# A second projection: unit loads ahead of the bias stores, token tiles' steps in another order

## The chip, the cores and the metric

One core of a Trainium2 chip runs the whole program. The metric is the device time of one execution in microseconds. The engines are TensorE (PE; PEld is its weight load), VectorE (DVE), ScalarE (ACT), GpSimd (POOL) and SyncE (SP), which here issues nearly all transfers from one queue, in program order.

## What is computed

Two transformer blocks on 512 tokens of width 1024, in fp32. The first block is a projection, stick-breaking attention and a recurrent scan, and a mixture of 32 experts; the second takes its normed output, projects it to queries, keys, values and gates, and does windowed attention. What matters here lies between the two:

```python
h = h + y.reshape(B, S, D)              # experts' rows are added
x = rmsnorm(h, final_norm_g)            # end of the first block
h = rms_norm(x, norm_gain[layer])       # start of the second
proj = h @ w_in[layer]                  # 1024 x 8448
qa, ka, va, qb, kb, vb, ga, gb, mg = jnp.split(proj, split_idx, axis=-1)
bias = bias_table[t5_bucket(rel * stride)]    # relative position bias of the attention
```

## The kernel before

The stage at issue is the class `SecondProjection`. Its weights come in 21 units of 256 columns and 1 MB each. Each is loaded raw by SyncE, then split into a high part (ScalarE, L653) and a low part (VectorE, L661), and TensorE multiplies three products of the parts (high by high, high by low, low by high). Unit 0 has a raw room of its own; the others alternate between two rooms, so that the load of unit n waits until the low part of unit n - 2 is made. The parts alternate between two rooms also, but unit 2 has a third one.

Ahead of that the tokens are prepared in four tiles of 128. For each tile c the rows of the two chosen experts are loaded into `yg` (1 MB, L2222), added to `h` in two additions (`add(c, 0)`, `add(c, 1)`, L2390, VectorE), squared and summed (`square(c)`, L2324, ScalarE), weighed with the squared gains (`weigh(c)`, L2395, VectorE), and turned into a diagonal of scales (`scale(c)`, to L2408, VectorE, with two roots on ScalarE). TensorE then turns the tile with it (`turn(c)`, L2245, 16 matmuls), ScalarE makes eight high parts (`highs(c)`, L2338) and VectorE eight low parts (`low(c)`, L2413). TensorE multiplies tile by tile with units 0 and 1 (24 matmuls of 256 columns each, L2274); within unit 1, behind 18 of its 24 matmuls, stands the turning of the next tile. Then come units 2 to 20 one by one for all 512 tokens: two jobs of 24 x 2 or 24 matmuls each (L603), and after a job with a head norm two matmuls of head sums.

The bias rows (`BiasRows`) are made beside this: SyncE loads tables, TensorE picks rows of them (L2096), VectorE adds the windows (`add_windows`, L2105), SyncE stores them in four copies of 256 KB (`store`, L2112), from where attention reads them later. They lie in `qk_a`, the room of the first normed queries, so that VectorE waits for their landing before it writes there.

The order on every engine is that of the code: each engine's method issues its instructions one after the other, and a waiting instruction holds all behind it. On SyncE the method `sync` issues the units' loads, the row loads, the stores of the bias rows and four stores of values (L2233) in one line. On ScalarE and VectorE the splits of a unit stand at chosen places between the tiles' steps.

Of the kernel before, what the change touches and what calls it, by code (L numbers as in the profile page):

```python
# [17 lines left out]
TT = S // P  # L18
# [2129 lines left out]
class SecondProjection:  # L2148
# [65 lines left out]
    def sync(self, sp, rows_written):  # L2214
        T, wts, const = self.T, self.wts, self.const
        w, cols = second_columns(self.A)
        sp.dma_start(wts.slot(0), w[:, :, cols[0]:cols[0] + UNIT]).then_inc(const["second_w_in"], 16)
        sp.dma_start(self.fin_g[:, :], self.A["final_norm_g"].rearrange("(a d) -> a d", a=1).broadcast_to([P, D])).then_inc(self.gain_in, 16)
        wts.load(sp, 1)
        sp.wait_ge(*rows_written)  # L2220
        for c in range(TT):
            sp.dma_start(self.yg[c], self.rows[c]).then_inc(self.got[c], 16)  # L2222
        self.bias.load(sp)
        v_rows = T["v_dram"].rearrange("(c p) w -> p c w", p=P)
        early = 2 * HW // UNIT
        for u in range(2, len(wts.cols)):
            wts.load(sp, u)
            if u == 2:
                self.bias.store(sp)
            if 3 <= u < early + 3:  # L2230
                at = slice((u - 3) * UNIT, (u - 2) * UNIT)
                sp.wait_ge(self.v_st, self.plain.index(self.last_job[u - 3]) + 1)
                sp.dma_start(v_rows[:, :, at], T["v12"][:, :, at]).then_inc(T["v12_written"], 16)  # L2233
            if u == early + 4:
                sp.wait_ge(T["v12_written"], 16 * early)
                sp.wait_ge(self.bias.stored, 64)
                load_bias(sp, const, T["band0"], 0, 0, 3 * P, T["band0_in"])
# [76 lines left out]
    def scalar(self, act):  # L2314
        jobs, normed, bank, wts, const, sq, rs = self.jobs, self.normed, self.bank, self.wts, self.const, self.sq, self.rs
        act.preload_act_table(ACT.Sqrt)
        for u in range(self.EARLY):
            wts.split_high(act, u)

        def square(c):  # L2320
            act.wait_ge(self.added, 2 * c + 2)
            if c >= 2:
                act.wait_ge(self.weighed, c - 1)
            act.activation(self.h_sq[c % 2], self.h[:, c, :], ACT.Square, accum_out=self.ss[:, c:c + 1]).then_inc(self.squared, 1)  # L2324

        def highs(c):
            act.wait_ge(self.fin, 3 * c + 2)
            act.activation(self.ws[:, c:c + 1], self.ws[:, c:c + 1], ACT.Sqrt).then_inc(self.root, 1)
            act.wait_ge(self.fin, 3 * c + 3)
            act.activation(const["fin_rstd"][:, c:c + 1], self.inv[:, c:c + 1], ACT.Sqrt).then_inc(self.root, 1)  # L2330
            if c == 0:
                act.wait_ge(self.gains_made, 1)
            for k in range(KC):
                if k < self.NTURN:
                    act.wait_ge(self.turned, self.NTURN * c + k + 1)
                else:
                    act.wait_ge(self.low_st, KC * c + k - self.NTURN + 1)
                act.activation(self.hT[0][:, k, c * P:(c + 1) * P], self.turn_at(k), ACT.Copy, scale=self.fin_cols[:, k:k + 1]).then_inc(self.high_st, 1)  # L2338

        square(0)  # L2340
        for c in range(TT):
            if c + 1 < TT:
                square(c + 1)
            highs(c)
        act.preload_act_table_set("natural_log_exp_and_others")
        wts.split_high(act, self.EARLY)

        def factors(i):

            act.wait_ge(self.summed, i + 1)  # L2350
            if i >= 2:
                act.wait_ge(self.qk_st, i - 1)
            act.activation(rs[:, i % 2, :], self.sums[i % 2][:, :], ACT.Ln, scale=1.0 / HD, bias=const["eps"][:, :]).then_inc(self.logged, 1)
            act.wait_ge(self.logged, i + 1)
            act.activation(rs[:, i % 2, :], rs[:, i % 2, :], ACT.Exp, scale=-0.5).then_inc(self.rstd, 1)

        for n, (u, kind, x, dst, gain, perm) in enumerate(jobs):
            act.wait_ge(self.ready, n + 1)
            if n in normed:
                i = normed.index(n)  # L2360
                if i >= 2:
                    act.wait_ge(self.summed, i - 1)
                act.activation(sq[:, i % 2, :], bank[n % self.NBANK][:, :], ACT.Square).then_inc(self.hn_squared, 1)
                act.wait_ge(self.hn_squared, i + 1)
                act.activation(self.sq_part[0][:, i % 2, :], sq[:, i % 2, :], ACT.Copy).then_inc(self.sq_high, 1)  # L2365
            else:
                width = P if kind == "va" else UNIT
                act.activation(dst, bank[n % self.NBANK][:, :].rearrange("p (c w) -> p c w", w=width), ACT.Copy).then_inc(self.v_st, 1)
            if u >= self.EARLY and self.last_job.get(u - 1) == n - 1:
                wts.split_high(act, u + 1)  # L2370
            if n - 1 in normed:
                factors(normed.index(n - 1))
# [8 lines left out]
    def vector(self, dve):  # L2381
# [3 lines left out]
        def add(c, j):  # L2385
            if j == 0:
                dve.wait_ge(self.got[c], 16)
            else:
                dve.wait_ge(self.added, 2 * c + 1)
            dve.scalar_tensor_tensor(out=self.h[:, c, :], in0=self.yg[c][:, j, :], scalar=self.weights[:, j, c:c + 1], in1=self.h[:, c, :],  # L2390
                                     op0=ALU.mult, op1=ALU.add).then_inc(self.added, 1)
# [27 lines left out]
        wts.split_low(dve, 0)  # L2419
        dve.wait_ge(self.gain_in, 16)  # L2420
        dve.tensor_tensor(self.gain_sq, self.fin_g[:, :], self.fin_g[:, :], ALU.mult).then_inc(self.gained, 1)
        wts.split_low(dve, 1)
        dve.wait_ge(self.gained, 1)

        for c in range(2):
            for j in range(2):
                add(c, j)
        weigh(0)
        for c in range(TT):
            scale(c)  # L2430
            if c + 2 < TT:
                add(c + 2, 0)
            elif c + 1 < TT:
                weigh(c + 1)
            low(c)
            if c + 2 < TT:
                add(c + 2, 1)
                weigh(c + 1)
        wts.split_low(dve, self.EARLY)
        for c in range(TT):  # L2440
            dve.tensor_tensor(self.h[:, c, :], self.h[:, c, :], self.fin_g[:, :], ALU.mult).then_inc(self.gained, 1)
        self.bias.add_windows(dve)
        dve.wait_ge(self.bias.stored, 64)
        for m, (u, *_) in enumerate(jobs):
            if u >= self.EARLY and self.last_job.get(u - 1) == m - 1:
                wts.split_low(dve, u + 1)
# [2 lines left out]
                continue  # L2449
            u, kind, x, dst, gain, perm = jobs[n]  # L2450
            i = normed.index(n)
            dve.wait_ge(self.rstd, i + 1)
            r = rs[:, i % 2, :]
            dve.tensor_scalar(r, r, gains[:, gain:gain + 1], None, ALU.mult).then_inc(self.hn_gained, 1)
# [797 lines left out]
```

## Time and profile before

| | |
|---|---|
| median of 3 timed runs | 1354.25 us (1352.88 to 1354.81) |
| the profiled execution | 1351.7 us |
| its span, first to last instruction | 1350.0 us |
| TensorE busy | 1230.9 us, 91% of the span |
| TensorE weight loads busy | 967.8 us, 72% |
| VectorE busy | 559.8 us, 41% |
| ScalarE busy | 492.2 us, 36% |
| GpSimd busy | 153.8 us, 11% |

TensorE is the busy engine; a time gained or lost is one in which it stands still or runs at the lower clock. Busy shares are means over stages with different limits, so the stage at issue, from about 710 to 830 us, has to be read on its own: what TensorE waited for in it, and what that waited for.

### The profile page before, as it was taken

Reading aid. Unit: us, or ns where it says so; the run is one execution under the profiler, and the core shown is the slowest. Engines: PE = TensorE matmul, PEld = TensorE weight load, DVE = VectorE, ACT = ScalarE, POOL = GpSimd, SP = SyncE. Lnnn points to the kernel's source line nnn. Section 1 sums busy time; section 2 is a strip of 40 time slices with the busy share of each in tenths; the row PEclk is TensorE's granted clock in tenths of the full one; section 3 lists DMA queues with packets and bytes.
Section 4 is the critical chain, followed back from the end, with each engine's and each line's share of the span. In section 5 each row is a group of like instructions: output and inputs, shape, how many; then the busy total and the mean of one; then the engine's idle time right before and its main releaser. Section 6 shows DMA issues by size and latency. Waiting matters only on the chain. (4 is left out here: it accounts for less than half of the span.)

```text
span 1350.0 us, 24557 instructions
## 1 busy us (share of the span) xinstructions
PE 1230.9 (91%) x10443; PEld 967.8 (72%) x10443; DVE 559.8 (41%) x1018; ACT 492.2 (36%) x881; POOL 153.8 (11%) x210
## 2 busy tenths in 40 slices
PE   5999999999979779999782939999999999999988
PEld 5787765699858546565442938888896678888888
DVE  3433563345373323333226602344446773553242
ACT  4324537602243311111113414455546663332230
POOL 4000013200000011111100001122210015300000
PEclk9999999999999979999996969999999999999999
DMA  4431000000029699999987064422216118222031
GB/s 157 122 104 63 32 1 0 9 5 4 15 72 408 235 368 417 418 418 418 418 368 247 6 167 126 96 90 94 94 32 95 64 34 281 63 63 94 0 109 48
DMA packets 92679, 197.63 MB, mean 146 GB/s; under 512 B 9694, under 2 KB 73276, under 8 KB 79644
## 3 DMA queue, kind: packets, MB, share of 16 engines
q1 hardware_dynamic: 87244, 185.58, 39.2%
q0 software_dynamic: 4752, 8.40, 1.6%
q10 hardware_dynamic: 576, 2.10, 0.4%
q8 instruction: 83, 1.36, 0.4%
q14 instruction: 24, 0.20, 0.0%
HBM read 186.06 MB, written 17.86 MB: 151 GB/s over the span
## 5 line engine op out<-in xcount | busy, mean ns | idle before, releaser
L661 DVE TENSOR_TENSOR w_in_low<-w_in_raw,w_in_high 128x2048 fp32r<-128x2048 f32 x19 | 43.6, 2293 | 122.1 <-ACT w_in_high L653 122.1
L1945 PE MATMUL hidden_ps<-w_gate,gathered_t 128*64 128x256 f32 x384 | 90.4, 389 | 0.3 <-DVE gathered_t L2022 0.3
L1945 PE MATMUL hidden_ps<-w_up,gathered_t 128*64 128x256 f32 x384 | 90.3, 389 | 0.0
L1487 PE MATMUL wo_ps<-w_out_high,wo_x_high 128*128 128x256 f32 x256 | 74.2, 290 | 3.5 <-DVE w_out_low L672 3.5
L2862 PE MATMUL gate_ps<-block_in_high,gate_w_high 128*128 128x512 f32 x192 | 75.9, 395 | 1.0 <-PEq L2531 1.0
L2862 PE MATMUL gate_ps<-block_in_high,gate_w_low 128*128 128x512 f32 x192 | 74.9, 390 | 0.0
L2862 PE MATMUL gate_ps<-block_in_low,gate_w_high 128*128 128x512 f32 x192 | 74.8, 390 | 0.0
L1487 PE MATMUL wo_ps<-w_out_high,wo_x_low 128*128 128x256 f32 x256 | 73.1, 285 | 0.0
L1487 PE MATMUL wo_ps<-w_out_low,wo_x_high 128*128 128x256 f32 x256 | 73.0, 285 | 0.0
L1945 PEld LDWEIGHTS hidden_ps<-w_gate,gathered_t 128*64 128x64 f32 x384 | 51.6, 139 | 27.6 <-issue 2.1
L2379 POOL TENSOR_TENSOR qk_sq_low<-y_a_b,qk_sq_high 128x512 fp32r<-128x512 f32 x29 | 37.5, 1294 | 247.2 <-ACT qk_sq_high L2365 247.2
L603 PE MATMUL u_ps<-mixer_in_high,w_in_high 128*128 128x512 f32 x160 | 63.7, 398 | 1.7 <-DVE w_in_low L661 1.7
L603 PE MATMUL u_ps<-mixer_in_low,w_in_high 128*128 128x512 f32 x160 | 62.3, 390 | 0.0
L603 PE MATMUL u_ps<-mixer_in_high,w_in_low 128*128 128x512 f32 x160 | 62.3, 389 | 0.0
L2002 ACT ACTIVATE silu<-hidden_ps 64x256 f32<-64x256 f32 x32 | 12.0, 375 | 137.6 <-PE hidden_ps L1945 137.6
L1967 PE MATMUL expert_ps<-w_down,hidden 128*64 128x512 f32 x216 | 51.3, 595 | 8.9 <-issue 6.5
L2048 DVE TENSOR_TENSOR hidden_t<-hidden_ps,silu 64x256 f32<-64x256 f32 x32 | 13.7, 427 | 108.5 <-ACT silu L2002 108.5
L1487 PEld LDWEIGHTS wo_ps<-w_out_high,wo_x_high 128*128 128x128 f32 x256 | 49.5, 194 | 8.9 <-issue 5.0
L1945 PEld LDWEIGHTS hidden_ps<-w_up,gathered_t 128*64 128x64 f32 x384 | 51.6, 139 | 0.0
L1487 PEld LDWEIGHTS wo_ps<-w_out_high,wo_x_low 128*128 128x128 f32 x256 | 49.9, 195 | 0.0
L1487 PEld LDWEIGHTS wo_ps<-w_out_low,wo_x_high 128*128 128x128 f32 x256 | 49.5, 194 | 0.0
L653 ACT ACTIVATE w_in_high<-w_in_raw 128x2048 fp32r<-128x2048 f32 x19 | 36.2, 1903 | 24.4 <-DMA w_in_raw<-w_in_dram 24.4
(531 smaller groups left out, 3250.4 us busy)
## 6 DMA issues: line engine op xcount, KB each, us to landing
w_down<-exp_w_down_dram SPq DMA_DIRECT2D x27, 1024.0 KB, 28.0
w_gate<-exp_w_gate_dram SPq DMA_DIRECT2D x24, 1024.0 KB, 22.5
w_up<-exp_w_up_dram SPq DMA_DIRECT2D x24, 1024.0 KB, 25.1
w_in_raw<-w_in_dram SPq DMA_DIRECT2D x20, 1024.0 KB, 5.6
slot_scratch_and_keys<-w_in_dram SPq DMA_DIRECT2D x14, 1024.0 KB, 5.2
vb<-w_in_dram SPq DMA_DIRECT2D x6, 1024.0 KB, 5.7
gate_w_raw_odd<-w_in_dram SPq DMA_DIRECT2D x6, 1024.0 KB, 6.4
slot_scratch_and_keys<-exp_w_down_dram SPq DMA_DIRECT2D x5, 1024.0 KB, 30.6
```

The lines of the kernel that those rows point to most:

```text
L603: m = pe.matmul(out, a(k)[i], b(k)[j], start=(k == 0 and i + j == 0), stop=(k == n - 1 and i == 1))
L653: act.activation(self.part[0][self.at(n)], self.slot(n), ACT.Copy).then_inc(self.high, 1)
L661: dve.tensor_tensor(self.part[1][self.at(n)], self.slot(n), self.part[0][self.at(n)], ALU.subtract).then_inc(self.low, 1)
L1487: m = pe.matmul(banks[n % nb][:, 0:UNIT], x[a][k][:, c * P:(c + 1) * P], wts.parts(u, k, slice(0, UNIT))[b], start=(k == 0 and a + b == 0) ...
L1945: x = pe.matmul(g_bank[e % 2][a * CAP:(a + 1) * CAP, 0:DE], xT[e % 2][:, k, :], w[:, k, :], start=(k == 0), stop=(k == KC - 1))
L1967: x = pe.matmul(y_bank[e % 2][half * CAP:(half + 1) * CAP, :], hid[e % 2][:, f, :], wd[e % NBD][:, f, half * 512:(half + 1) * 512], start= ...
L2002: act.activation(act_g[e % 2][CAP:P, :], g_bank[e % 2][0:CAP, 0:DE], ACT.Silu).then_inc(silu, 1)
L2048: dve.tensor_tensor(hid_t[e % 2][CAP:P, :], g_bank[e % 2][CAP:P, 0:DE], act_g[e % 2][CAP:P, :], ALU.mult).then_inc(mul_r, 1)
L2379: pool.tensor_tensor(self.sq_part[1][:, 0, :], self.sq[:, i % 2, :], self.sq_part[0][:, i % 2, :], ALU.subtract).then_inc(self.sq_low, 1)
L2862: m = pe.matmul(bank[n % NBANK][:, :], wts.parts(unit, k, w)[a], hT[b][:, k, :], start=(k == 0 and a + b == 0), stop=(k == KC - 1 and a == 1))
```

## The change

It moves instructions and adds none. On SyncE the load of unit 1 goes behind the first row load, and the stores of the bias rows go from behind unit 2's load to behind unit 4's. On ScalarE the high part of unit 1 goes behind tile 0's high parts, and the square of tile c + 1 behind the high parts of tile c. On VectorE the second addition of tile c + 1 and its weighing go behind the low parts of tile c (for tile 1 the addition stays ahead of them), and unit 1's low part goes behind tile 0's. VectorE's wait for the bias rows' landing goes from behind the windows to ahead of the first head norm.

```diff
--- before.py
+++ after.py
@@ -2216,16 +2216,17 @@
         w, cols = second_columns(self.A)
         sp.dma_start(wts.slot(0), w[:, :, cols[0]:cols[0] + UNIT]).then_inc(const["second_w_in"], 16)
         sp.dma_start(self.fin_g[:, :], self.A["final_norm_g"].rearrange("(a d) -> a d", a=1).broadcast_to([P, D])).then_inc(self.gain_in, 16)
-        wts.load(sp, 1)
         sp.wait_ge(*rows_written)
         for c in range(TT):
             sp.dma_start(self.yg[c], self.rows[c]).then_inc(self.got[c], 16)
+            if c == 0:
+                wts.load(sp, 1)
         self.bias.load(sp)
         v_rows = T["v_dram"].rearrange("(c p) w -> p c w", p=P)
         early = 2 * HW // UNIT
         for u in range(2, len(wts.cols)):
             wts.load(sp, u)
-            if u == 2:
+            if u == self.EARLY + 2:
                 self.bias.store(sp)
             if 3 <= u < early + 3:
                 at = slice((u - 3) * UNIT, (u - 2) * UNIT)
@@ -2314,8 +2315,7 @@
     def scalar(self, act):
         jobs, normed, bank, wts, const, sq, rs = self.jobs, self.normed, self.bank, self.wts, self.const, self.sq, self.rs
         act.preload_act_table(ACT.Sqrt)
-        for u in range(self.EARLY):
-            wts.split_high(act, u)
+        wts.split_high(act, 0)
 
         def square(c):
             act.wait_ge(self.added, 2 * c + 2)
@@ -2339,9 +2339,11 @@
 
         square(0)
         for c in range(TT):
-            if c + 1 < TT:
-                square(c + 1)
+            if c:
+                square(c)
             highs(c)
+            if c == 0:
+                wts.split_high(act, 1)
         act.preload_act_table_set("natural_log_exp_and_others")
         wts.split_high(act, self.EARLY)
 
@@ -2419,28 +2421,28 @@
         wts.split_low(dve, 0)
         dve.wait_ge(self.gain_in, 16)
         dve.tensor_tensor(self.gain_sq, self.fin_g[:, :], self.fin_g[:, :], ALU.mult).then_inc(self.gained, 1)
+        dve.wait_ge(self.gained, 1)
+
+        add(0, 0)
+        add(0, 1)
+        add(1, 0)
+        weigh(0)
+        scale(0)
+        add(1, 1)
+        low(0)
         wts.split_low(dve, 1)
-        dve.wait_ge(self.gained, 1)
-
-        for c in range(2):
-            for j in range(2):
-                add(c, j)
-        weigh(0)
-        for c in range(TT):
+        for c in range(1, TT):
+            weigh(c)
             scale(c)
-            if c + 2 < TT:
-                add(c + 2, 0)
-            elif c + 1 < TT:
-                weigh(c + 1)
+            if c + 1 < TT:
+                add(c + 1, 0)
             low(c)
-            if c + 2 < TT:
-                add(c + 2, 1)
-                weigh(c + 1)
+            if c + 1 < TT:
+                add(c + 1, 1)
         wts.split_low(dve, self.EARLY)
         for c in range(TT):
             dve.tensor_tensor(self.h[:, c, :], self.h[:, c, :], self.fin_g[:, :], ALU.mult).then_inc(self.gained, 1)
         self.bias.add_windows(dve)
-        dve.wait_ge(self.bias.stored, 64)
         for m, (u, *_) in enumerate(jobs):
             if u >= self.EARLY and self.last_job.get(u - 1) == m - 1:
                 wts.split_low(dve, u + 1)
@@ -2449,6 +2451,8 @@
                 continue
             u, kind, x, dst, gain, perm = jobs[n]
             i = normed.index(n)
+            if i == 0:
+                dve.wait_ge(self.bias.stored, 64)
             dve.wait_ge(self.rstd, i + 1)
             r = rs[:, i % 2, :]
             dve.tensor_scalar(r, r, gains[:, gain:gain + 1], None, ALU.mult).then_inc(self.hn_gained, 1)
```

SyncE at the row loads: `slot_scratch_and_keys` holds raw unit 0, `w_in_raw` the later raw units, `qb` and `vb` the experts' rows (`yg`).

```order
 L2218 DMA final_gain<-final_norm_g_dram 128x1024
-L642 DMA w_in_raw<-w_in_dram 128x8x256
-L2220 REGISTER_ALU
-L2222 DMA qb<-expert_rows_dram 128x2048 x3
-L2222 DMA vb<-expert_rows_dram 128x2048
+L2219 REGISTER_ALU
+L2221 DMA qb<-expert_rows_dram 128x2048
+L642 DMA w_in_raw<-w_in_dram 128x8x256
+L2221 DMA qb<-expert_rows_dram 128x2048 x2
+L2221 DMA vb<-expert_rows_dram 128x2048
```

The load of unit 1 moved from ahead of the wait for the experts' rows to between the first and the second row load.

SyncE behind the bias tables' loads: `bias_rows_dram` are the bias rows' stores, `class_v_dram` the values' stores.

```order
 L2091 DMA sink<-sink_a_dram 128x8
+L642 DMA w_in_raw<-w_in_dram 128x8x256 x2
+L2234 DMA class_v_dram<-vb 128x4x256
 L642 DMA w_in_raw<-w_in_dram 128x8x256
 L2112 DMA bias_rows_dram<-qk_a 128x1x512 x4
```

Units 2, 3 and 4 and the first values' store now stand ahead of the bias rows' stores, where only unit 2 stood.

VectorE between the low parts of tile 0 and of tile 1: `block_in_low` are the tokens' low parts, `h<-` the additions, the ISA rows the weighing, `y_a_b<-ident` the diagonal for turning. Before:

```order
L2413 SCALAR_TENSOR_TENSOR block_in_low<-expert_ps,final_gain_columns,block_in_high 128x128 x2
L2390 SCALAR_TENSOR_TENSOR h<-qb,route_weights,h 128x1024
L2395 ISA vb,fin_weighted<-vb 128x1024
L2395 ISA fin_weighted 128x1
L2400 TENSOR_SCALAR fin_squares<-fin_squares 128x1
```

Of the change:

```order
L2415 SCALAR_TENSOR_TENSOR block_in_low<-expert_ps,final_gain_columns,block_in_high 128x128 x2
L661 TENSOR_TENSOR w_in_low<-w_in_raw,w_in_high 128x2048
L2397 ISA vb,fin_weighted<-vb 128x1024
L2397 ISA fin_weighted 128x1
L2402 TENSOR_SCALAR fin_squares<-fin_squares 128x1
```

Unit 1's low part, which stood ahead of the first addition, now stands behind tile 0's low parts and ahead of tile 1's weighing, and the addition of tile 2 there has gone behind the diagonal.

## Rows read from the trace of the kernel before

**Rows 1.** Waits of TensorE, whole run: instruction, what it waited for: us, times, longest.

```profile
PE hidden_ps L603 <- DVE w_in_low L661: 20.8, 1, 20.8
```

**Rows 2.** Timeline of SyncE: start, us, engine, line, operation, output<-input, count.

```profile
718.38 1.29 SPq L2222 DMA_DIRECT2D qb<-expert_rows_dram  x3
...
771.58 10.05 SPq L2112 DMA_DIRECT2D bias_rows_dram<-qk_a  x4
781.67 3.78 SPq L642 DMA_DIRECT2D w_in_raw<-w_in_dram  x1
```

**Rows 3.** Timeline of ScalarE, units 2 to 5; in brackets: idle before it, releaser.

```profile
772.57 0.60 ACT L2368 ACTIVATE vb<-expert_ps 128x512 f32<-128x512 f32 x1 [4.86 <-PE expert_ps L603]
794.37 1.91 ACT L653 ACTIVATE w_in_high<-w_in_raw 128x2048 fp32r<-128x2048 f32 x1 [21.20 <-DMA w_in_raw<-w_in_dram]
...
807.17 0.60 ACT L2368 ACTIVATE vb<-hidden_ps 128x512 f32<-128x512 f32 x1 [10.41 <-PE hidden_ps L603]
...
812.93 0.60 ACT L2368 ACTIVATE vb<-hidden_ps 128x512 f32<-128x512 f32 x1 [3.37 <-PE hidden_ps L603]
818.40 0.60 ACT L2363 ACTIVATE y_a_b<-hidden_turned_ps 128x512 f32<-128x512 f32 x1 [4.87 <-PE hidden_turned_ps L603]
...
819.56 1.90 ACT L653 ACTIVATE w_in_high<-w_in_raw 128x2048 fp32r<-128x2048 f32 x1
```

**Rows 4.** Timeline of VectorE, bias windows and unit 3.

```profile
770.29 1.27 DVE L2105 TENSOR_TENSOR qk_a<-gathered_ps,qk_a 16x512 f32<-16x512 f32 x2
796.40 2.29 DVE L661 TENSOR_TENSOR w_in_low<-w_in_raw,w_in_high 128x2048 fp32r<-128x2048 f32 x1 [24.85 <-ACT w_in_high L653]
```

**Rows 5.** Stretch of the stores: us, TensorE busy (matmuls), clock, DMA share, GB/s.

```profile
776.00:778.00 2.00, 1.97 (x18) 1.00 0.44 48
```

**Rows 6.** DMA issues near 781, 718.4 and 718.9 us: count, size, us to landing.

```profile
w_in_raw<-w_in_dram SPq DMA_DIRECT2D x1, 1024.0 KB, 12.6
...
qb<-expert_rows_dram SPq DMA_DIRECT2D x1, 1024.0 KB, 6.1
...
qb<-expert_rows_dram SPq DMA_DIRECT2D x1, 1024.0 KB, 8.2
```

**Rows 7.** Timeline of VectorE, tiles 0 and 1.

```profile
725.09 5.12 DVE L2390 SCALAR_TENSOR_TENSOR h<-qb,route_weights,h 128x1024 f32<-128x1024 f32 x4
730.12 1.22 DVE L2395 CUSTOM_DVE_ANT_0 vb<-vb 128x1024 f32<-128x1024 f32 x1
...
739.09 1.22 DVE L2395 CUSTOM_DVE_ANT_0 vb<-vb 128x1024 f32<-128x1024 f32 x1
...
744.74 0.60 DVE L2413 SCALAR_TENSOR_TENSOR block_in_low<-expert_ps,final_gain_columns,block_in_high 128x128 fp32r<-128x128 f32 x2
```

**Rows 8.** Timeline of TensorE: the first matmuls of the turns of tiles 0 to 2.

```profile
732.49 2.08 PE L2245 MATMUL gathered_ps<-y_a_b,h 128*128 128x128 f32 x8 [23.40 <-DVE y_a_b L2408]
...
741.46 1.16 PE L2245 MATMUL gathered_ps<-y_a_b,h 128*128 128x128 f32 x8 [0.24 <-DVE y_a_b L2408]
...
749.11 1.05 PE L2245 MATMUL gathered_ps<-y_a_b,h 128*128 128x128 f32 x8
```

**Rows 9.** Timeline of ScalarE, tile 0's last high parts, a later square.

```profile
736.96 0.64 ACT L2338 ACTIVATE block_in_high<-expert_ps,final_gain_columns 128x128 fp32r<-128x128 f32 x2
...
746.57 1.06 ACT L2324 ACTIVATE vb<-h 128x1024 f32<-128x1024 f32 x1 [1.61 <-DVE h L2390]
747.53 0.19 ACT L2324 ACTIVATION_READ_ACCUMULATOR vb<-h 128x1 f32 x1
```

**Rows 10.** TensorE behind two gaps (timeline), and the stretches there (columns of rows 5).

```profile
398.34 2.05 PE L593 MATMUL wo_ps<-heads 128*128 128x128 f32 x8 [3.01 <-PEq L102]
...
463.56 0.43 PE L1657 MATMUL router_in_ps<-ident,router_in_t 36*128 36x36 f32 x4 [2.56 <-DVE router_in_t L1680]
...
398.00:399.00 1.00, 0.66 (x3) 0.50 0.00 0
463.00:464.00 1.00, 0.43 (x4) 1.00 0.98 406
```

## The prediction

> **What bounds the kernel now.** I read first the table of waits of TensorE over the whole run. Its second-longest entry is 20.8 us, once, in the first matmul of a weight unit of the second projection: it waits for VectorE's low part [rows 1]. To see what that wait hangs on I followed it back through three timelines. VectorE makes the low part of unit 3 at 796.40 [rows 4], ScalarE its high part at 794.37, after idling 21.2 us for the transfer of the raw unit [rows 3]. SyncE issues that transfer at 781.67, directly behind the four stores of the bias rows, which occupied it from 771.58 for 10.05 us [rows 2]. They were last released by VectorE's addition of the windows (770.29, two of them, 1.27 us together [rows 4]). The room that unit 3 is loaded into was free since unit 1's low part, before 725.09 [rows 7]. So the order on one queue holds TensorE, and nothing else does: that is what the change can win.
>
> **Part 1, unit 3 (and 4) ahead of the stores.** The load of unit 3 waits for two low parts, now made before tile 1 is turned; the load of unit 4 waits for unit 2's low part, made before the windows are added. Both are then on their way before 771.6 in the old times. What is late next? ScalarE has the copy of unit 2's first result at 772.57 [rows 3]; behind it comes unit 3's high part, 1.91 us [rows 3], and VectorE's low part, 2.29 us [rows 4], no longer behind the wait for the stores' landing, which the change moves to the first head norm. 772.6 + 0.6 + 1.9 + 2.3 = 777.4. TensorE ended unit 2 about 798.75 - 20.8 = 777.95. The 20.8 us go whole, with 0.5 us to spare.
>
> With them goes a cold start: unit 3's first job ran from 798.75 to 807.17, 8.4 us, the second, alike, took 812.93 - 807.17 = 5.76 us [rows 3]; the difference, 2.6 us, is gone if TensorE does not stop. Part 1 gives **-23.4 us**.
>
> What it delays is unit 5, now the first load behind the stores. Its need in old times: unit 3 ends at 777.95 + 2 x 5.76 = 789.5; unit 4's first job takes 818.40 - 812.93 = 5.47 [rows 3] and ends at 795.0; the high part starts 819.56 - 818.40 = 1.2 us later [rows 3], and could start 0.8 us later still, since TensorE has two head sums between unit 4 and unit 5. So unit 5 must have landed by 796.2 to 797.0. Unit 3's load took 12.6 us from its issue right behind the stores [rows 6], landing at 794.3. Ahead of unit 5's load there is half a megabyte more, a store of values; a megabyte took about 2.5 us on a busy queue (landings of 6.1 and 8.2 us for two row loads issued about 0.4 us apart [rows 6]), so 1.3 us more: 795.6. I cost this at **zero**, with 3 us as the other bound, the cover being 0.6 to 1.4 us.
>
> Why that load is slow shows in the stores' stretch: the DMA engines' mean busy share was 0.44 at 48 GB/s [rows 5]. By a rule of the Trainium skill (DMA: Bandwidth & Descriptors, Rules for kernel authors) a copy whose outermost dimension is under 16, here 8 heads, is confined to at most that many of the engines. The trace agrees, with a share just under a half; a load behind the stores must then wait on those engines, which speaks against putting any load there, and the change still leaves unit 5's.
>
> **Part 2, row loads.** Unit 1's load goes from before the wait on the experts' rows to behind the first row load. Tile 0's chain starts when the rows land. Before, the first was issued at 718.38 [rows 2] and landed 6.1 us later, at 724.5, the second 8.2 us after its issue, at 727.0 [rows 6]; VectorE added four half-rows from 725.09 and weighed at 730.12 [rows 7]. Now only three additions stand ahead, but the third needs the second row load, and unit 1's megabyte is between the two. Set against the old order the same bytes have moved when it lands, and the DMA engines stand idle while SyncE waits for the rows, for an estimated 1 to 2 us. So it lands at 727.0 + 1.3 = 728.3, addition three ends at 729.6, weighing starts then instead of 730.12: **-0.5 us**. Bounds: -1.8 (no idle time, 727.0) and +2.5 (the first row load still takes 6.1 us, then two megabytes at 2.5 us: 729.5, and up to 731.3 if unit 1's smaller packets run slower, which gives weighing at 732.6).
>
> **Part 3, tiles.** Let T be TensorE's first turning matmul, 732.49 now [rows 8]. Unit 1's split is no longer made before T but after tile 0's high parts on ScalarE and low parts on VectorE. The last high parts start at 736.96 and two more take 0.64 [rows 9], so they end at T + 5.1. ScalarE then takes 1.91 for unit 1 (T + 7.0), VectorE 2.29 (T + 9.3). TensorE had its 24 matmuls of unit 0 done at about T + 6.2 and must stand 3.1 us, which it did not before. VectorE goes on with tile 1: its weighing (ScalarE's square is done by T + 8.0) starts at T + 9.2. From weighing to turning takes 741.46 - 739.09 = 2.37 us [rows 7, 8] and 732.49 - 730.12 says the same. So tile 1 is turned at T + 11.6; before it was 741.46 - 732.49 = 8.97. **+2.6 us.**
>
> For tiles 2 and 3 the order is now turn, low parts, second addition, square, weigh, turn, in a chain without overlap, because the sum of a tile is completed only after the previous tile's low parts. Turn to low parts' end: 744.74 + 0.60 - 741.46 = 3.9 [rows 7, 8]. From there to weighing: addition 1.25 (four took 5.12 [rows 7]), square from 746.57 to 747.53 + 0.19 [rows 9], in all 2.4. Then 2.37. Sum 8.65 from turn to turn. Before it was 749.11 - 741.46 = 7.65 [rows 8], with TensorE busy throughout. Two such steps, of 1.0 and (the old step to tile 3 was 0.1 shorter) 1.1: **+2.1 us**. Behind the last turn all goes as before, shifted. Part 3 is 4.7 us.
>
> **Part 4, the clock.** A gap of 3.01 us in this trace was followed by a stretch at a granted clock of 0.50, the 1.2 GHz level; one of 2.56 us was not (1.00, 2.4 GHz) [rows 10]. The new gap of 3.1 us is on the side of the first. I take it that the clock falls. The 18 matmuls of unit 1 before the turn need 18/64 of a 7.6 us step, 2.1 us, and twice that at the lower level; TensorE then reaches the turn at T + 13.5 instead of T + 11.6: **+2.0 us** (bounds 0, and 2.6, what the first job lost after 20.8 us of idling).
>
> The Trainium skill (TensorE: Matmul & The Clock Gate, Part 1: The HAM clock gate) says that the point of change varies from run to run, since the gate's phase is not tied to the kernel. By that rule term 4 may be 0 in some executions and 2.0 in others, so it would be no fixed cost; no run seen so far shows it for this place.
>
> **Sum.** -23.4 - 0.5 + 4.7 + 2.0 = -17.2 us. The profiled execution took 1351.7 us (span 1350.0), so it would take 1334.5. The three timed runs have a median of 1354.25, 2.55 above it; I forecast the median, 1354.25 - 17.2 = **1337.0 us**.
>
> **Rivals.** (a) The clock does not fall in tile 0, and the rest holds: 1335.0. For it: 2.56 us was tolerated. Chance 0.25. (b) Transfers come late: the second row load by up to 2.5 us, or unit 5 by up to 3; 1339 to 1342. For it: both covers are about 1 us, and the estimates rest on one transfer each. Chance 0.18. (c) Slower. The clock, low at T, never comes back while the tiles have gaps: a tile then costs about twice 7.6, three steps +23, the matmuls behind the last turn +6, unit 2 (two jobs of 5.76) +11.5, and unit 3's cold start stays: 1354.25 + 40.5 - 20.8 - 0.5 = 1373. It decides at this point: the 20.8 us are used up when the clock is still low at the last turn; if it returns in tile 0 or 1, the kernel wins. Against it: it returned before tile 1 in the old order, and in the new one the gaps behind tile 1 are only 1 us. Chance 0.02. (d) The change does not do what it says: unit 3 is gated by something that the transfer hid, as a wait of ScalarE or VectorE; up to 20.8 us come back, at most 1360, and 1354 if most does. Against it: each of its waits is named above and met by 777.4. Chance 0.03, half of it within 0.2%, which is about what a measurement of this kernel can tell from no change.
>
> The forecast itself has 0.52, with its own range of 1335 to 1339. The range that leaves 0.2 out or less reaches from (a) with the row loads at their best, 1335.0 - 1.3 and a scatter of a microsecond or two between runs, 1332.0, to the upper end of (b), 1342.0. Faster 0.96, same 0.01, slower 0.03.
>
> **What the new profile would show.** No wait of 20 us in the projection and SyncE's stores behind two more unit loads: part 1. A wait of 3.1 us for unit 1's low part behind the first 24 matmuls, then two of about 1 us for the turning diagonal, with turns 8.65 us apart: part 3. A granted clock of 0.5 right behind the 3.1 us: part 4. TensorE's first turn at 732.0: part 2. The prediction is wrong if TensorE waits over 3 us at unit 3 or 5, or if the turns are closer than 8.

## The result

The changed kernel took 1335.98 us (median of four runs, 1332.8 to 1337.4); the kernel before took 1354.53 beside it. The ratio of the two is 0.9861, with a 95% interval of 0.984 to 0.9883: 18.6 us less. The forecast was 1337.0, with a range of 1332 to 1342. The profiled execution took 1337.41 us, its span is 1335.7.

The waits of TensorE from 700 to 1020 us in the changed kernel (instruction, what it waited for: us in all, times, longest), the answer to [rows 1]:

```profile
PE gathered_ps L2246 <- DVE y_a_b L2410: 24.1, 3, 22.4
PE attn_score_ps L2627 <- PEq L102: 2.1, 1, 2.1
PE hidden_ps L2275 <- DVE w_in_low L661: 1.8, 1, 1.8
...
PE expert_ps L603 <- DVE w_in_low L661: 0.3, 1, 0.3
```

The 20.8 us of [rows 1] are gone. New are 1.8 us in unit 1 (L2275), two waits for the turning diagonal (24.1 less 22.4 is 1.7 in two), and 0.3 us at unit 5.

SyncE's timeline (start, us, line, operation, output<-input, count), to be held against [rows 2]:

```profile
722.12 0.34 SPq L2221 DMA_DIRECT2D qb<-expert_rows_dram  x1
722.50 0.43 SPq L642 DMA_DIRECT2D w_in_raw<-w_in_dram  x1
...
774.09 0.37 SPq L642 DMA_DIRECT2D w_in_raw<-w_in_dram  x1
780.07 10.06 SPq L2112 DMA_DIRECT2D bias_rows_dram<-qk_a  x4
790.17 3.75 SPq L2234 DMA_DIRECT2D class_v_dram<-vb  x1
793.97 2.35 SPq L642 DMA_DIRECT2D w_in_raw<-w_in_dram  x1
```

The stores take SyncE as long as before, 10.06 us, and are followed by the load of unit 5 at 793.97 instead of that of unit 3. On ScalarE (against [rows 3]) unit 3's high part at 781.55 follows unit 2's first result at once, and unit 5's at 805.23 waits half a microsecond for its transfer:

```profile
781.05 0.60 ACT L2370 ACTIVATE vb<-expert_ps 128x512 f32<-128x512 f32 x1 [4.86 <-PE expert_ps L603]
781.55 1.91 ACT L653 ACTIVATE w_in_high<-w_in_raw 128x2048 fp32r<-128x2048 f32 x1
...
803.46 0.60 ACT L2365 ACTIVATE y_a_b<-hidden_turned_ps 128x512 f32<-128x512 f32 x1 [4.87 <-PE hidden_turned_ps L603]
...
805.23 1.92 ACT L653 ACTIVATE w_in_high<-w_in_raw 128x2048 fp32r<-128x2048 f32 x1 [0.50 <-DMA w_in_raw<-w_in_dram]
...
815.36 0.60 ACT L2365 ACTIVATE y_a_b<-expert_ps 128x512 f32<-128x512 f32 x1 [3.96 <-PE expert_ps L603]
```

TensorE's turns, the answer to [rows 8], and the first matmul of unit 1, which waited 1.78 us:

```profile
736.06 2.08 PE L2246 MATMUL gathered_ps<-y_a_b,h 128*128 128x128 f32 x8 [22.40 <-DVE y_a_b L2410]
745.47 0.39 PE L2275 MATMUL hidden_ps<-w_in_high,block_in_high 128*128 128x256 f32 x1 [1.78 <-DVE w_in_low L661]
...
747.72 1.14 PE L2246 MATMUL gathered_ps<-y_a_b,h 128*128 128x128 f32 x8
...
756.36 1.16 PE L2246 MATMUL gathered_ps<-y_a_b,h 128*128 128x128 f32 x8 [0.86 <-DVE y_a_b L2410]
...
765.03 1.16 PE L2246 MATMUL gathered_ps<-y_a_b,h 128*128 128x128 f32 x8 [0.86 <-DVE y_a_b L2410]
```

**A ruler for the stage.** The experts' stage ahead of this one ends at a different time in every execution, whatever the kernel: unit 0's load was issued between 707.2 and 715.0 us in the profiles below, at 709.98 in that of the kernel before and at 714.56 here. Times are therefore counted from that issue. The columns are read from the timelines of SyncE, TensorE and ScalarE: the first turn, from the first to the second and to the last turn, and the copy of unit 5's first result, up to which all that the change touches has happened. The last column is the median of the runs, with that of the kernel before beside it.

| kernel | first turn | to second | to last | unit 5's first result | median, before beside it |
|---|---|---|---|---|---|
| before | 22.51 | 8.97 | 24.16 | 119.75 | 1354.53 |
| changed | 21.50 | 11.66 | 28.97 | 100.80 | 1335.98, 1354.53 |
| e1_loads_only | 23.72 | 9.66 | 24.74 | 98.73 | 1331.73, 1352.27 |
| e2_tiles_only | 21.68 | 11.65 | 28.95 | 123.64 | 1355.99, 1352.27 |
| e3_wait_kept | 21.79 | 11.66 | 28.98 | 117.76 | 1353.11, 1352.27 |
| e4_two_stores | 23.35 | 9.57 | 24.65 | 115.68 | 1348.49, 1352.27 |
| e5_change_again | 21.83 | 11.65 | 28.96 | 101.11 | 1337.79, 1354.34 |
| e6_unit1_early | 22.09 | 11.66 | 28.97 | 101.82 | 1335.52, 1354.34 |
| e7_all | 21.29 | 9.10 | 24.27 | 95.25 | 1330.32, 1354.34 |
| e8_tile0_first | 18.96 | 10.12 | 27.43 | 96.16 | 1330.13, 1354.34 |
| e9_change_warm | 23.00 | 10.90 | 28.58 | 101.81 | 1335.98, 1356.77 |
| e10_all_warm | 26.50 | 7.26 | 22.44 | 98.60 | 1335.23, 1356.77 |
| e11_all_short_warm | 22.72 | 7.26 | 22.44 | 94.82 | 1327.13, 1352.57 |
| e12_all_again | 22.63 | 9.09 | 24.27 | 96.56 | 1329.44, 1352.57 |

By this ruler the change is worth 119.75 - 100.80 = 18.95 us, close to the 18.6 of the medians, and splits into these parts: first turn -1.0, turns +4.8, from unit 2's first result to unit 4's (772.57 to 818.40 before, 781.05 to 803.46 now) -23.4, unit 5 +0.6 (11.90 instead of 11.33 us behind unit 4's first result), 0.1 between. The first two parts scatter: in e1_loads_only and e4_two_stores, whose order of the tiles is that of the kernel before, the first turn came at 23.72 and 23.35 instead of 22.51, and the turns took 24.74 and 24.65 instead of 24.16. Against those two kernels the turns of the changed one cost 4.2 to 4.3 us.

### The profile page after: what moved, and what is told of

Read it like the earlier page. It is cut to its first block and busy times, and to the rows that moved or that the text cites. A ratio compares the mean times of both kernels' runs of the same rounds, so it can differ in the third digit from the quotient of the medians.

```text
span 1335.7 us, 24557 instructions
## 1 busy us (share of the span) xinstructions
PE 1235.7 (93%) x10443; PEld 968.3 (72%) x10443; DVE 560.2 (42%) x1018; ACT 492.3 (37%) x881; POOL 154.0 (12%) x210
## 5 line engine op out<-in xcount | busy, mean ns | idle before, releaser
L661 DVE TENSOR_TENSOR w_in_low<-slot_scratch_and_keys,w_in_high 128x2048 fp32r<-128x2048 f32 x14 | 32.1, 2292 | 26.5 <-ACT w_in_high L653 26.4
```

The lines of the kernel that those rows point to most:

```text
L661: dve.tensor_tensor(self.part[1][self.at(n)], self.slot(n), self.part[0][self.at(n)], ALU.subtract).then_inc(self.low, 1)
```

## Experiments

### One half without the other

The kernel before with the queue order alone:

```diff
-            if u == 2:
+            if u == self.EARLY + 2:
                 self.bias.store(sp)
...
-        dve.wait_ge(self.bias.stored, 64)
...
+            if i == 0:
+                dve.wait_ge(self.bias.stored, 64)
```

> The kernel before with two edits only: the bias rows' stores behind unit 4's load, and VectorE's wait for their landing ahead of the first head norm. The token tiles keep their old order and unit 1's load its old place. Theory (the gain is the queue order alone, the tiles' new order costs about 4 us): no wait at unit 3, 23.4 us less, about 0.6 us back at unit 5, so 1354.5 - 22.8 = 1331.7 us, some 4 us below the changed kernel. Rival (the tiles' new order is needed, since the early load of unit 3 or the split of unit 1 stands in the way of something in the old order): no faster than the changed kernel, 1336 us or more.

Measured: 1331.73 us. That it meets the expected 1331.7 is partly luck: the sum behind that number starts from 1354.5, and beside this run the kernel before took 1352.27, so 20.5 us went and not 22.8. Of TensorE's waits in the stage only the first turn's and unit 5's 0.3 us are left. By the ruler it takes 98.73 against 100.80 us, 2.1 less than the change, not 4, since the first turn came later here (23.72) while the turns were 4.2 us shorter together.

The complement, the changed kernel with SyncE's order and VectorE's wait as before:

```diff
-            if u == self.EARLY + 2:
+            if u == 2:
                 self.bias.store(sp)
...
+        dve.wait_ge(self.bias.stored, 64)
...
-            if i == 0:
-                dve.wait_ge(self.bias.stored, 64)
```

> The changed kernel with the stores and VectorE's wait put back where they were: only the reordered tiles and the moved load of unit 1 are left. Theory: the first turn comes 1.0 us earlier, the last turn 4.9 us later than it did relative to the first, so 3.9 us more than before, 1358.4 us, with the wait of 20.8 us at unit 3 as it was. Rival (the reordering gains something by itself, for instance an earlier unit 3): 1354.5 us or less.

Measured: 1355.99 us beside 1352.27, 3.7 more; the ratio's interval, 0.9988 to 1.0047, does not exclude no change, but the trace does: 123.64 against 119.75 us, 3.9 more, and the old wait whole:

```profile
PE hidden_ps L603 <- DVE w_in_low L661: 20.9, 1, 20.9
PE hidden_ps L2275 <- DVE w_in_low L661: 2.4, 1, 2.4
```

So the whole gain is the queue's order, with VectorE's wait moved behind it (below), and the tiles' new order costs about 4 us, as the sum had it.

### The moved wait of VectorE

The changed kernel with `dve.wait_ge(self.bias.stored, 64)` back behind the windows:

```diff
         self.bias.add_windows(dve)
+        dve.wait_ge(self.bias.stored, 64)
...
-            if i == 0:
-                dve.wait_ge(self.bias.stored, 64)
```

> The changed kernel with VectorE's wait for the stores' landing put back behind the windows, ahead of unit 3's low part; SyncE's order is that of the change. Theory (the wait was covered by the late load and would be next): the stores start at 780.1 and their slow stretch ends at about 794 in the changed kernel's trace, so unit 3's low part starts at about 795 instead of 783.6 and TensorE stands about 11 us, with 2.6 us for the cold start behind it: 1336.0 + 13.5 = 1349.5 us. Rival (the wait costs nothing, moving the stores was all): 1336.0 us.

Measured: 1353.11 us; nearly the whole gain is lost. VectorE's waits from 760 to 810 us name the stores:

```profile
DVE w_in_low L661 <- DMA bias_rows_dram<-qk_a: 19.2, 1, 19.2
```

and TensorE's waits from 690 to 1020 us the unit behind them:

```profile
PE hidden_ps L603 <- DVE w_in_low L661: 15.1, 1, 15.1
```

The mechanism is the expected one, and the size was wrong: 11 us of waiting were expected, 15.1 came. The stores, issued from 777.43, had landed only at 796.6, 19.2 us later; about 14 had been expected. In the kernel before this wait cost nothing: stores that take as long would have landed by 771.58 + 19.2 = 790.8 (an estimate), while unit 3's transfer landed at 794.3 [rows 2, 6] and its low part started at 796.40 [rows 4]. One wait hid the other: with the stores moved and the wait left, 2.0 of the 19 us by the ruler remain (117.76 against 119.75).

### Why the stores are slow

The kernel before, storing the bias rows in two copies of 16 partitions:

```diff
-        for g in range(4):
-            a, b = divmod(g, 2)
-            sp.dma_start(self.const["bias_dram"][g], self.tab[b * NH:(b + 1) * NH, a:a + 1, :].broadcast_to([NH, SKEW, 512])).then_inc(self.stored, 16)
+        for a in range(2):
+            sp.dma_start(self.const["bias_dram"][2 * a:2 * a + 2].rearrange("b h s x -> (b h) s x"),
+                         self.tab[0:2 * NH, a:a + 1, :].broadcast_to([2 * NH, SKEW, 512])).then_inc(self.stored, 16)
```

> The kernel before with one edit: the bias rows are stored in two copies of 16 partitions instead of four of 8; the same bytes, the same place. Theory (the stores are slow because a copy with 8 outermost rows runs on at most half of the DMA engines): the busy share in their stretch doubles from 0.44 to about 0.9, SyncE is through in about 5 us instead of 10, and the load of unit 3 lands 8 to 9 us earlier: the wait of 20.8 us falls to about 12, about 1346 us. Rival (the stores are slow for another reason, such as the packets' writes to memory): share and time as before, 1354.5 us.

A stretch of 2 us in the stores (us, TensorE busy with its matmuls, clock, DMA share, GB/s), the answer to [rows 5]:

```profile
780.00:782.00 2.00, 1.66 (x15) 1.00 0.90 98
```

The landing of a store and of unit 3's load, both under way at 776.7 us (count, size, us to landing):

```profile
w_in_raw<-w_in_dram SPq DMA_DIRECT2D x1, 1024.0 KB, 15.5
bias_rows_dram<-qk_a SPq DMA_DIRECT2D x1, 512.0 KB, 12.1
```

The share went from 0.44 to 0.90 and the rate from 48 to 98 GB/s, both twice as high with twice the rows in a copy. That part of the theory holds, though the number of copies was halved with the same edit, and no run has one without the other; the rule of the Trainium skill cited in the prediction (DMA: Bandwidth & Descriptors, Rules for kernel authors) agrees with both shares. The gain did not follow in size: TensorE's wait fell from 20.8 to 15.0, not to 12, and the median by 3.8 us, not 8.5. SyncE was through with the stores in 1.35 us instead of 10.05 and issued unit 3's load 1.4 us behind the first store instead of 10.1, but the load then took 15.5 us to land instead of 12.6 [rows 6]. Counted from the first store it landed at 16.9 us instead of 22.7, 5.8 us earlier, which is what the wait lost. The second store had landed 12.8 us behind the first one's issue, so most of the load's time went by behind the stores. The expectation had counted the earlier issue as gained in full. By the ruler 4.1 us are left (115.68 against 119.75), mostly because the first turn (0.8) and the turns (0.5) came later here than in the one profile of the kernel before.

### Unit 1's load

The changed kernel unedited, and with unit 1's load back ahead of the wait for the experts' rows:

```diff
+        wts.load(sp, 1)
         sp.wait_ge(*rows_written)
         for c in range(TT):
             sp.dma_start(self.yg[c], self.rows[c]).then_inc(self.got[c], 16)
-            if c == 0:
-                wts.load(sp, 1)
```

> The changed kernel once more, unedited, on the chip of this comparison, as the yardstick for the three beside it and for a second look at tile 0's clock. By the first four runs: 1336.0 us. Theory of term 4 (the clock did not fall in tile 0 because the cold start outlasted unit 0's matmuls and the gap shrank to about 2 us): no stretch at 0.50 behind that gap again. Rival (it was luck of this one execution, and the clock falls in half of them): a stretch at 0.50 behind the gap.

> The changed kernel with one edit: unit 1's load goes back ahead of the wait for the experts' rows; all else as changed. It isolates part 2. Theory (unit 1's megabyte competes with the experts' last row writes: the rows were released 8.4 to 9.2 us after unit 0's load in the three kernels that have it there and 7.6 to 7.7 in the three that have it behind): the first row load goes out 1.0 to 1.5 us later, the second lands at about 18.8 us after unit 0's load against 17.9, and the first turn comes 0.8 us later, so 1336.8 us. Rival of the first prediction (with the rows' loads side by side the third addition no longer waits, 1.8 us won over the kernel before's first turn): first turn at 20.7 us after unit 0's load, 1.0 us earlier than changed, 1335.0 us.

The unedited kernel took 1337.79 us, the edited one 1335.52; 2.3 us apart the wrong way for the theory, but the four runs of each spread over more than 5 us, and the traces have it: first turn at 21.83 and 22.09, 0.3 us apart. VectorE's additions in the edited kernel:

```profile
723.06 3.80 DVE L2391 SCALAR_TENSOR_TENSOR h<-qb,route_weights,h 128x1024 f32<-128x1024 f32 x3 [4.63 <-DMA qb<-expert_rows_dram]
```

All three run in a row, where in the changed kernel the third waited 2.79 us for the second row load. But the first row load, issued 9.0 us after unit 0's load instead of 7.6 to 7.7, lands at 15.9 instead of 12.5 to 12.6 us. The two effects cancel to 0.3 us. In the four profiles with the load in its new place and these tiles (the two of the changed kernel, e2_tiles_only and e3_wait_kept) the first turn came at 21.5 to 21.8 us, so 22.09 in one profile is hardly outside their scatter. Moving this load is worth next to nothing as long as the third addition stands ahead of the first weighing; the rival with 1.0 us fell, and of the theory's 0.8 us a third was seen.

### Better orders

The loads-only kernel with two stores, and tile 0 weighed behind three additions:

```diff
-        for c in range(2):
-            for j in range(2):
-                add(c, j)
+        add(0, 0)
+        add(0, 1)
+        add(1, 0)
         weigh(0)
         for c in range(TT):
             scale(c)
+            if c == 0:
+                add(1, 1)
```

> The loads-only kernel (old tile order) with two more edits: tile 0 is weighed behind three additions instead of four, ScalarE squaring tile 1 behind tile 0's high parts; and the bias rows go out in two stores of 16 partitions. Theory: one addition less ahead of the first turn, 1.2 us; the store's slow stretch shrinks from 19 to 12 us, so unit 5's transfer is in time and 0.6 us go too: 1331.7 - 1.8 = 1329.9 us, TensorE's waits in the stage being the first turn's alone. Rival (the addition taken from ahead of the first turn comes back ahead of the second, as VectorE has no slack between turns): a wait of about 1 us at tile 1's turn, and 1331 us.

Measured: 1330.32 us, and 1329.44 in a second comparison (expected of it):

> The kernel e7_all once more, unedited, as the yardstick beside it: 1330.3 us, second turn 9.1 us behind the first.

Unit 5 is in time (its first result 11.36 us behind unit 4's, as in the kernel before), TensorE has no wait in the stage but the first turn's, and the stage is 3.5 and 2.2 us shorter than that of the loads-only kernel: 0.6 at unit 5, 0.5 in the turns, and 2.4 and 1.1 at the first turn, where one addition less was expected to give 1.2. The ratios to the kernel before, 0.9821 and 0.9828 against 0.9819 for the loads-only kernel, do not tell them apart. The rival's wait at tile 1 was not there in one profile and 0.2 us in the other.

The other way round, the changed kernel with tile 0 weighed ahead of tile 1's first addition, unit 1's high part ahead of tile 0's, and two stores:

```diff
         add(0, 0)
         add(0, 1)
-        add(1, 0)
         weigh(0)
         scale(0)
+        add(1, 0)
         add(1, 1)
...
+            if c == 0:
+                wts.split_high(act, 1)
+                act.wait_ge(self.gains_made, 1)
...
-            if c == 0:
-                wts.split_high(act, 1)
```

> The changed kernel with three edits: tile 0 is weighed behind its own two additions, ahead of tile 1's first; ScalarE splits unit 1 ahead of tile 0's high parts; two stores of 16 partitions. Theory: the first turn no longer hangs on the second row load. The first landed 12.5 us after unit 0's load in the changed kernel, so the turn comes at 12.5 + 6.2 = 18.7 instead of 21.5 us, 2.8 earlier; unit 1's low part starts right behind tile 0's low parts, 1.5 us earlier; unit 5 is in time, 0.6: 1336.0 - 4.9 = 1331.1 us, level with the loads-only kernel. Rival (the second row load is needed just as early for tile 1 and the chain from tile to tile of 8.65 us eats the lead): 1334 us or more.

Measured: 1330.13 us, and by the ruler 4.6 us less than the change (96.16), where 4.9 were expected: first turn at 18.96, second 10.12 us behind it. It shows what putting unit 1 behind the first row load could be good for, once nothing ahead of the first turn needs the second row load. The slower steps from tile to tile, 27.43 against 24.27, take the lead back.

### The clock in tile 0

Term 4 forecast a fall of the clock behind a gap of 3.1 us. Neither profile of the changed kernel has one, nor have e2_tiles_only, e3_wait_kept and e6_unit1_early, which have the same tile order. In the changed kernel's first profile (columns as in [rows 5], stretches of 1 us):

```profile
741.00:742.00 1.00, 1.00 (x7) 0.54 0.40 126
...
743.00:744.00 1.00, 0.69 (x6) 1.00 0.00 0
744.00:745.00 1.00, 0.00 (x0) 1.00 0.00 0
745.00:746.00 1.00, 0.54 (x4) 1.00 0.00 0
```

The clock came back at 741.9 (a mean of 0.54 from 741 to 742 is 0.08 us at the upper level), only 5.9 us behind the first turn, against 3.4 in the kernel before and 3.8 to 6.0 in the others up to e8_tile0_first and in e12_all_again. Unit 0's matmuls so ended later and the gap was 1.8 us (2.45 in the second profile, where the clock came back after 4.4). To get the gap that the forecast had, 32 matmuls whose results are overwritten go ahead of the first turn, in the changed kernel and in e7_all:

```diff
+        wts.wait(pe, 0)
+        pe.wait_ge(self.added, 1)
+        keep_busy(pe, const, self.turn_bank[0], 32)
         self.turn(pe, 0)
```

> The changed kernel with 32 extra matmuls of 128 columns on TensorE ahead of tile 0's turning, whose results are overwritten; they start when tile 0's first addition is done, some 7 us before the first turn. It takes the cold start out of tile 0 and so makes the gap behind unit 0's matmuls as long as the prediction had it. Theory: at the higher clock the low parts of tile 0 end 3.9 us behind the turn instead of 5.5, so the second turn comes 10.1 instead of 11.6 us behind the first, 1.5 us less in all; unit 0's matmuls end at 4.7 us and TensorE stands about 3.1 us. If term 4 of the prediction was right about such a gap, the granted clock falls to 0.50 behind it and the 1.5 us are lost again; rival: it stays at 1.00 and 1.5 us are won, 1336.0 - 1.5 = 1334.5 us.

> The kernel e7_all with the same 32 extra matmuls. Here no gap follows. Theory (the cold start costs tile 0 about 1.5 us, since turning, high and low parts run at the pace of the turning matmuls): the second turn 7.6 us behind the first instead of 9.1, 1330.3 - 1.5 = 1328.8 us. Rival (VectorE's additions and weighing between the turns are the bound, not the matmuls): second turn still about 9 us behind, no gain, 1330.3 us.

In both the extra matmuls ran 9.2 us, longer than the 7.5 and 4.8 us from their start to the diagonal that the first turn needs. They held the first turn back by 1.5 and 4.3 us, so the medians (1335.98 and 1335.23) say nothing of the clock. The traces do. TensorE's timeline in the changed kernel with them, unit 1's first matmul and the second turn:

```profile
745.60 0.39 PE L2278 MATMUL hidden_ps<-w_in_high,block_in_high 128*128 128x256 f32 x1 [2.71 <-DVE w_in_low L661]
...
748.93 1.50 PE L2246 MATMUL gathered_ps<-y_a_b,h 128*128 128x128 f32 x8
```

and the stretches there:

```profile
745.00:746.00 1.00, 0.40 (x3) 1.00 0.00 0
746.00:747.00 1.00, 1.00 (x8) 0.72 0.44 49
747.00:748.00 1.00, 1.00 (x7) 0.50 0.61 186
```

With TensorE at the 2.4 GHz level from the first turn on, the gap grew to 2.71 us, and behind it the granted clock did fall to 0.50: the second turn came 10.90 us behind the first. In the changed kernel it came 2.25 us behind unit 1's first matmul (747.72 - 745.47). Here 745.60 + 2.25 would be 9.8 us behind the first turn (VectorE's diagonal was ready by then, at 747.78), so 1.1 us were lost. The third turn came another 9.01 us later instead of 8.64, 0.4 more. The fall is real in this execution, and it cost about 1.4 us. In e10_all_warm there is no gap behind unit 0's matmuls and no fall, and the second turn comes 7.26 us behind the first, against 9.10: the cold start costs tile 0 1.8 us.

Whether such a gap always brings a fall is another matter. The gap of 2.56 us ahead of the router's matmuls, which the prediction took as one that the clock tolerates [rows 10], is there in every trace, as long to within 0.01 us. In the kernel before and in e7_all the clock stayed at 1.00 behind it. In the changed kernel's first profile and in e8_tile0_first it fell 0.9 to 1.0 us later, TensorE idling again. In the ten others it fell within the gap or within 0.1 us of its end, as in e12_all_again (TensorE's timeline, and stretches with the columns of [rows 5]):

```profile
465.59 0.64 PE L1657 MATMUL router_in_ps<-ident,router_in_t 36*128 36x36 f32 x4 [2.56 <-DVE router_in_t L1680]
...
465.00:466.00 1.00, 0.41 (x4) 0.81 1.02 422
466.00:467.00 1.00, 0.23 (x3) 0.50 0.99 410
```

With 13 extra matmuls instead of 32:

> The kernel e10_all_warm with 13 extra matmuls instead of 32. The 32 took 9.2 us and held the first turn back by 4.3 us; the time between the first addition and the first turn is 4.8 us, of which the first 3.6 go at the lower clock, so 13 should just fill it. Theory: first turn as in e7_all (21.3 us after unit 0's load, less with earlier rows), second turn 7.3 us behind it as in e10_all_warm, against 9.1: 1330.3 - 1.8 = 1328.5 us. Rival (the extra matmuls only shift the cold start, the clock falls back or rises late): second turn 9 us behind the first, no gain over e12_all_again.

Measured: 1327.13 us beside 1329.44 for e7_all again in the same comparison, the stage 94.82 against 96.56 us. The runs spread from 1325.3 to 1333.9, so the medians alone do not settle the 1.8 us; the second turn at 7.26 us against 9.09 does. The clock was back 0.3 us ahead of the first turn, and the first turn, held back by 0.7 us, came at 22.72 against 22.63. It has the lowest median and the shortest stage of all kernels tried, though its ratio to the kernel before, 0.9832 (0.9797 to 0.9867), cannot be told from those of e7_all, 0.9821 and 0.9828, e8_tile0_first, 0.9816, and e1_loads_only, 0.9819. By the length of the stage all of them beat both the kernel before and the changed one.

## Why the prediction was right

The median came out 1.0 us below the forecast of 1337.0. The large term and the price of the tiles were right in mechanism and size; the term for the clock was not, and that the total is as close as it is owes something to luck: the misses in the small terms and the scatter of the medians made up for half of it.

**Bound and part 1.** The chain of one queue was read right: -23.4 us forecast, -23.4 measured between unit 2 and unit 4, with the cold start of unit 3 gone as well. That the wait of VectorE had to move with the stores was named as a step, and e3_wait_kept shows it to be worth 17 us.

**Unit 5** was costed at nothing with 3 us as the bound, its landing being due by 796.2 to 797.0 and forecast at 795.6 in old times. It took 0.6 us. The load landed 11.2 us behind its issue at 793.97, at 805.2; all else had shifted by 8.5, so in old times that is 796.7, half a microsecond behind the 796.2 at which it was due. The estimate of the landing was 1.1 us early.

**Part 2**: -0.5 forecast, -1.0 measured in the one profile, -0.7 in the second. The difference is in the rows' release, which the step did not have: the first row load went out 7.56 us behind unit 0's load instead of 8.40. In every profile with unit 1's load ahead of it this took 8.4 to 9.2 us, in every one with unit 1's load behind it 7.6 to 7.7. The second row load landed 9.5 us behind its issue, close to the 728.3 - 718.9 = 9.4 of the forecast. The kernel before scatters at this place by itself, 22.5 to 23.7 us in the three kernels with its order there.

**Part 3**: +4.7 forecast, +4.8 measured; second turn at 11.6 forecast and 11.66 measured, steps of 8.65 forecast and 8.64 and 8.67 measured. This is what a chain worked out from a trace's own durations can give when every link is there. The old step of 8.97 us that it was held against was itself one execution; 9.66 and 9.57 in e1_loads_only and e4_two_stores would make it 4.2 and 4.3.

**Part 4** is the term that failed: +2.0 forecast, 0 measured. Its faulty step was that unit 0's matmuls are done at T + 6.2, taken from the one execution of the kernel before, in which the clock returned 3.4 us behind T. It returned at 5.9, the matmuls ended at 7.6, and the gap was 1.8 us, not 3.1. The gap's end was right (9.4 us behind T, 9.3 forecast). A gap of 2.71 us at this place was followed by a fall in the one profile of e9_change_warm, at a price of about 1.4 and not 2.0. The other step, that 3.01 us brings a fall and 2.56 us does not, was one execution of two different places; the same gap of 2.56 us had the fall in most of the later traces. The prediction's caution that the term may be 0 in some executions and not in others fits that better than its fixed cost. Rival (a) had described what happened, at 1335.0.

By the ruler the change is worth 18.95 us against 17.2 forecast: 2.0 from the clock, 0.5 from the first turn, less 0.6 at unit 5 and 0.1 each in the turns and behind them. The medians, 18.6 apart from the one before beside them and 18.3 from the one that the sum started from, hide part of that in their scatter. The other rivals fell: the reordered tiles did not slow the kernel beyond their 4.8 us, and no second gate held unit 3.

## What to carry to other kernels

When a wait goes, list every other wait of the instruction behind it, with the time at which each would have been met: the transfer hid a wait for the stores that was nearly as long. A change made of two edits should be summed as two: here one gave 21 to 23 us and the other cost 4, and either is easy to have alone. And where the start of a stage scatters by more than the effect sought, count from an event inside the stage. A threshold read from two gaps in one execution is no threshold: look at the same place in further executions before giving it a price.

## What was not expected of the hardware

The clock's return after a long idle time came 3.4 to 6.0 us behind the first turn in kernels whose matmuls there are the same, and it moves the length of the gap behind it. Gaps of 1.8 to 2.45 us at that place left the clock at the upper level in five profiles, and one of 2.71 us did not. At the router the same gap of 2.56 us was followed by no fall in the kernel before and in e7_all and by one in ten other profiles, so the length of a gap alone does not decide. Four stores of 256 KB had landed 19.2 us behind the first issue, at a DMA share of 0.44 to 0.48 while they had the queue; two stores of 512 KB had landed after 12.8 us, at 0.90.
